# Expert gate and up weights loaded two column blocks at a time in 2 MB transfers, and the pieces taken in a new order

## What is computed

```python
    logits = (xt @ router).astype(jnp.float32)
    top_vals, top_idx = lax.top_k(logits, TOP_K)
    gates = jax.nn.softmax(top_vals, axis=-1)
    ...
    for e in range(N_EXPERTS):
        y_e = swiglu(xt, w_gate[e], w_up[e], w_down[e])
        y = y + combine[:, e:e + 1] * y_e.astype(jnp.float32)
```

## Time and profile before

| | |
|---|---|
| median of 3 runs | 1504.56 us (1502.7 to 1506.28) |
| profiled execution, first to last instruction | 1504.0 us |
| DVE busy | 1331.8 us, 89% |
| ACT busy | 1107.7 us, 74% |
| PE busy (its ends are modelled) | 1418.1 us, 94% |
| weights and other reads | 460.79 MB, 308 GB/s over the span |
| TensorE clock, mean granted | 0.981 |

### The profile page before, as it was taken

The page is one execution under the profiler, slowest core; times in us unless marked ns, Lnnn a source line. Parts: engine busy times, 40 slices in busy tenths (PEclk is TensorE's granted clock), DMA queues, the critical chain, the costliest instruction groups (busy, mean ns, idle before and its releaser), DMA issues.

```text
span 1504.0 us, 40039 instructions
## 1 busy us (share of the span) xinstructions
PE 1418.1 (94%) x17659; PEld 1161.2 (77%) x17659; DVE 1331.8 (89%) x1324; ACT 1107.7 (74%) x1036; POOL 111.0 (7%) x160
## 2 busy tenths in 40 slices
PE   7999999999999999899999999999999889898786
PEld 5888878888888788698687797788777776766663
DVE  4999987545569899899999999999999999999997
ACT  4797755444358676587897878888888888978884
POOL 2121014000043001200000000000000000000001
PEclk8999999999999999999999999999999999999898
DMA  9654466457554527879999999999999999999993
GB/s 316 237 168 155 162 235 219 141 183 236 171 180 141 172 87 270 345 304 380 405 413 392 412 411 397 411 409 394 411 407 410 412 406 411 411 401 410 411 396 132
DMA packets 141347, 464.86 MB, mean 309 GB/s; under 512 B 8234, under 2 KB 10410, under 8 KB 126800
## 3 DMA queue, kind: packets, MB, share of 16 engines
q1 hardware_dynamic: 138960, 457.21, 79.7%
q0 software_dynamic: 1920, 4.55, 1.0%
q10 hardware_dynamic: 288, 0.48, 0.1%
HBM read 460.79 MB, written 2.89 MB: 308 GB/s over the span
## 4 chain that ended last, share of the span: by engine, by line
PE 56%; DVE 29%; DMA 5%; issue 4%; ACT 3%; POOL 1%; SPq 1%; DVEq 0%; ACTq 0%
PE ps L859 17%; PE ps L860 17%; PE ps L861 17%; DVE w_lo L2274 13%; DVE w_lo L2277 6%; ACT w_hi L1655 2%; PE ps L972 2%; DMA x<-in_moe_w_gate 2%; DMA stage<-in_w_in 2%; DMA stage<-in_moe_w_up 1%; DVE w_lo L1746 1%; POOL x L786 1%; DVE arena L2292 1%; DVE arena L2312 1%; SPq L646 1%
## 5 line engine op out<-in xcount | busy, mean ns | idle before, releaser
L861 PE MATMUL ps<-arena,w_lo 128*128 128x128 f16 (+7 forms) x3952 | 568.9, 215 | 13.7 <-issue 13.6
L859 PE MATMUL ps<-arena,w_hi 128*128 128x128 f16 (+7 forms) x3952 | 569.1, 215 | 13.4 <-issue 6.6
L860 PE MATMUL ps<-arena,w_hi 128*128 128x128 f16 (+7 forms) x3952 | 569.1, 215 | 11.3 <-issue 11.3
L859 PEld LDWEIGHTS ps<-arena,w_hi 128*128 128x128 f16 x3952 | 388.3, 100 | 28.9 <-issue 16.9
L860 PEld LDWEIGHTS ps<-arena,w_hi 128*128 128x128 f16 x3952 | 388.2, 100 | 25.1 <-issue 16.5
L861 PEld LDWEIGHTS ps<-arena,w_lo 128*128 128x128 f16 x3952 | 388.2, 100 | 12.8 <-issue 6.9
L859 PE MATMUL ps<-xhl,w_hi 128*128 128x264 f16 x1120 | 312.0, 279 | 11.8 <-DVE w_lo L1746 4.6
L860 PE MATMUL ps<-xhl,w_hi 128*128 128x264 f16 x1120 | 311.9, 278 | 0.0
L861 PE MATMUL ps<-xhl,w_lo 128*128 128x264 f16 x1120 | 311.8, 278 | 0.0
L1746 DVE SCALAR_TENSOR_TENSOR w_lo<-stage,w_hi 128x2048 f16<-128x2048 f32 (+1 forms) x95 | 210.5, 2236 | 81.7 <-ACT w_hi L1352 81.4
L1352 ACT ACTIVATE w_hi<-stage 128x2048 f16<-128x2048 f32 (+1 forms) x95 | 174.5, 1853 | 88.1 <-PE ps L861 75.3
(11 more groups left out here) (345 smaller groups left out, 1937.1 us busy)
## 6 DMA issues: line engine op xcount, KB each, us to landing
stage<-in_moe_w_up SPq DMA_DIRECT2D x57, 1024.0 KB, 14.0
stage<-in_moe_w_down SPq DMA_DIRECT2D x56, 1024.0 KB, 14.4
stage<-in_w_in SPq DMA_DIRECT2D x43, 1024.0 KB, 5.5
mixer_only<-in_moe_w_up SPq DMA_DIRECT2D x39, 1024.0 KB, 13.1
stage<-in_moe_w_gate SPq DMA_DIRECT2D x33, 1024.0 KB, 8.4
arena<-in_moe_w_gate SPq DMA_DIRECT2D x32, 1024.0 KB, 13.4
mixer_only<-in_moe_w_gate SPq DMA_DIRECT2D x24, 1024.0 KB, 13.7
x<-in_moe_w_down SPq DMA_DIRECT2D x16, 1024.0 KB, 14.8
```

What stands on the lines that cost most here:

```text
L859: mm(out, ah, bh, start=start, stop=False, skip_group_check=True)
L860: mm(out, ah, bl, start=False, stop=False, skip_group_check=True)
L861: return mm(out, al, bh, start=False, stop=stop, skip_group_check=True)
```

## The change

Gate and up are now loaded two blocks side by side: one load holds 256 rows of the matrix and 2048 columns (blocks 0 and 1, 2 MiB) or 1536 columns (blocks 2 and 3, 1.5 MiB); a load of down holds 512 rows (2 MiB), which is two of its pieces. An expert is 23 loads (`LOADS`) instead of 42, into seven homes of 2 MiB instead of 14 of 1 MiB, and a load waits until the last piece that reads the load seven places back is converted (`LAST_OF`). The pieces that ACT, DVE and PE work on have the size and number they had, but since a load serves two blocks, these are taken in turns, and `visit_order` becomes: gate of blocks 0 and 1 in turns (m = 0 to 7), up of the two in turns (8 to 15), gate of blocks 2 and 3 in turns (16 to 21), down of 0 and 1 (22 to 29), up of 2 and then 3 (30 to 35), down of 2 and 3 (36 to 41). ACT's and DVE's steps on the hidden values move to fixed m. A gate or up piece's rows no longer lie side by side in its home. ACT still writes `w_hi` of such a piece in one instruction (two for block 3); DVE writes `w_lo` in one instruction for each group of 128 rows, which is two for blocks 0 to 2 and four for block 3. The expert's tokens for the next visit are gathered ahead of m = 36 (before: ahead of m = 40). `FP32_DOWN` is empty, so that nothing is multiplied unsplit. Some tensors are laid side by side in memory (`zx`, `mixer_xhl`) to make 2 MiB homes of them.

```diff
--- before.py
+++ after.py
-RING = 14
-
-
-TWICE = 5
-RING_ORDER = list(range(TWICE, 12)) + list(range(TWICE)) + [12, 13]
+
+BIG = 2 * PIECE
+HOMES_AFTER = [2, 3, 4, 0, 1, 5, 6]
...
+SIDE = [2048, D_EX - 2048]
 def visit_order():
...
+    def in_turn(kind, b):
+        return [(kind, i, q) for part in range(2) for i in (b, b + 1)
+                for q in range(part * n_pieces(i) // 2, (part + 1) * n_pieces(i) // 2)]
+
+    def whole(kind, *blocks):
+        return [(kind, i, q) for i in blocks for q in range(n_pieces(i))]
+
+    return (in_turn("g", 0) + in_turn("u", 0) + in_turn("g", 2) + whole("d", 0, 1) + whole("u", 2, 3)
+            + whole("d", 2, 3))
...
+LOADS = ([("g", 0, q) for q in range(4)] + [("u", 0, q) for q in range(4)] + [("g", 1, q) for q in range(4)]
+         + [("d", 0, c) for c in range(4)] + [("u", 1, q) for q in range(4)] + [("d", 0, c) for c in range(4, NC)])
...
+LAST_OF = [max(m for m in range(VISIT) if j in loads_of(m)) for j in range(NLOADS)]
+
+FP32_DOWN = ()
...
+        HOMES = [stage[:, (PRE + i) % SLOTS:(PRE + i) % SLOTS + 2, :].rearrange("p i c -> p (i c)") for i in (0, 2, 4)] + [
+            mixer_only[:, 0:BIG], landing, mixer_xhl[:, BIG:2 * BIG], zx[:, 0:BIG]]
...
+        def halves_of(at, m, to, both=False):
+
+            kind, b, q = order[m]
+            slot = to[:, (PRE + m) % SLOTS, :]
+            if kind == "d":
+                return [(load_home(at, loads_of(m)[0])[:, (q % 2) * PIECE:(q % 2 + 1) * PIECE], slot)]
+            width = 512 * len(BLOCKS[b])
+            c0, side = (BLOCKS[b][0] * 512) % 2048, SIDE[b // 2]
+            k = KT // n_pieces(b)
+            dst = slot.rearrange("p (two k c) -> p two k c", two=2, k=k)
+            if both:
+                return [(load_home(at, j)[:, 0:2 * side].rearrange("p (k n) -> p k n", k=2)[:, :, c0:c0 + width]
+                         .rearrange("p k (c two) -> p two k c", two=2), dst[:, :, 2 * i:2 * i + 2, :])
+                        for i, j in enumerate(loads_of(m))]
+            return [(load_home(at, j)[:, t * side + c0:t * side + c0 + width].rearrange("p (c two) -> p two c", two=2),
+                     dst[:, :, 2 * i + t, :]) for i, j in enumerate(loads_of(m)) for t in range(2)]
...
+            kind, side, q = LOADS[j]
             if kind == "d":
-                return (A["moe_w_down"][0, e, f + q * 256:f + q * 256 + 256, :]
-                        .rearrange("a (p k) n -> (a p) k n", p=P)), 2, D
+                return (A["moe_w_down"][0, e, q * 512:q * 512 + 512, :]
+                        .rearrange("a (q p k) n -> (a p) q (k n)", p=P, k=2)), PIECE
...
+                        if first and i < 9:
+                            new_home(i)
+                        elif i < 7:
+                            sp.wait_ge(*in_visit(bank_full, 5, (r, 0), -1))
                         else:
-                            sp.wait_ge(S["lo_done"], so_far((r, v), VISIT, split(n - RING + 1)))
-                        load(*visit_piece(e, m), n + v * VISIT + (0 if first else ROUND))
-
-            def new_home(m):
-
-                if m < SLOTS:
-                    sp.wait_ge(S["lo_done"], split(PRE + m - SLOTS + 1))
-                elif m == SLOTS:
+                            was = ((r, (i - 7) // NLOADS), (i - 7) % NLOADS)
+                            load_used(*was)
...
+                if i < 3:
+                    sp.wait_ge(S["lo_done"], split(PRE + 2 * i + 2 - SLOTS))
+                elif i == 3:
                     filled(sp, ("so", L - 1))
-                elif m == 9:
+                elif i == 4:
                     sp.wait_ge(S["out_dma"], 16 * 11 * L)
-                elif m == 10:
+                elif i in (5, 6):
+                    load_used((0, 0), i - 5)
...
+                for m, (kind, blk, q) in enumerate(order):
+                    if kind == "d":
+                        down(at, blk, q)
+                    else:
+                        gate_up(at, kind, blk, q)
+                    if m == 7:
+                        scatter(at, 0)
+                    if m == 11:
+                        scatter(at, 1)
+                    if m == 15:
+                        select_rows(at, first)
+                    if last and m == 25:
+                        residual_rows(0, [tokens_added(at, 1), in_visit(bank_free, 7, at, 0)])
+                    if m == FP32_FROM - 1:
+                        if last:
+                            residual_rows(1, [columns_read("u", 2, at), columns_read("g", 3, at)])
+                        else:
+                            gather((at[0], at[1] + 1), at)
...
+                if n >= PRE:
+                    for j in loads_of(n - PRE):
+                        act.wait_ge(*load_landed((0, 0), j))
+                    piece_done(act, n - SLOTS)
+                    hi_of((0, 0), n - PRE)
...
+                parts = halves_of(at, m, w_hi, True)
+                for src, dst in parts[:-1]:
+                    fn(dst, src, ACT.Copy, scale=WS)
+                src, dst = parts[-1]
+                fn(dst, src, ACT.Copy, scale=WS).then_inc(S["hi_done"], 1)
...
+            def lo_of(at, m):
+
+                parts = list(zip(halves_of(at, m, w_lo), halves_of(at, m, w_hi)))
+                for (src, dst), (_, hi) in parts[:-1]:
+                    V.scalar_tensor_tensor(dst, src, WS, hi, ALU.mult, ALU.subtract)
+                (src, dst), (_, hi) = parts[-1]
+                V.scalar_tensor_tensor(dst, src, WS, hi, ALU.mult, ALU.subtract).then_inc(S["lo_done"], 1)
...
+                    if m == 24:
+                        select((at[0], v + 1))
+                    if m == 33:
+                        hidden(at, 2, silu_e, silu_e)
+                    if m == 34 and split_all:
+                        hidden_lo(at, 2, silu_e)
+                    if m == 35:
+                        hidden(at, 3, h_fp32[:, 3:4, :], h_fp32[:, 3:4, :])
+                    if m == 36 and split_all:
+                        hidden_lo(at, 3, h_fp32[:, 3:4, :])
...
```

521 lines of the change are left out of this document (272 added, 249 removed).

## The result

The changed kernel takes 1549.07 us (median of 4 runs, 1546.99 to 1550.39) against 1504.9: ratio 1.0289, 95% interval 1.0274 to 1.0304. It is 44 us slower, and 7 us above the top of my range. The direction was right; the size was near double what I had forecast.

What follows compares the result with a forecast made beforehand. DVE was taken to bound visits 4 to 6, PE mainly visits 0, 2 and 3, DMA second. Terms 7.3 + 2.5 - 2.3 + 6.6 + 3.3 + 5 + 1 = +23.4 took 1504.6 to 1528 us; range 1505 to 1542.

Steps and rivals of the forecast that it cites:

- DVE's extra instructions: w_lo on DVE: 36 more instructions a visit at 0.068 us; +7.3 in visits 4 to 6, +2.5 in 1 and 3.
- The higher figure of the Trainium skill: Fixed latency per DVE instruction: about 150 cycles, 0.16 us; 288 added instructions would be an estimated 45 us before cover.
- The start: First expert load: ACT held 4.4 us with the merged parts behind it, PE covering about 1.1 us; +3.3 us.
- The visit's end: Visit boundaries: PE's six last down pieces wait for block 2's rest part, DVE then waits 1.1 us; +6.6 over six.
- the tail: After the last w_lo: PE ends 10.7 us behind DVE, 5.9 more than before; taken as +5 us, no cover.
- the clock: PE's granted clock falls after gaps ahead of m = 36 in light visits; +1 us in all.
- Loads: Longer rows land faster, so visit 7's load waits vanish: -2.3 us there; later-freed homes cost 0.
- rival 1: Expert visits: loads are the true bound, longer rows save 15 us and hide DVE's instructions; 1498 us, 8%.
- Rival 3: Visit boundaries: homes come late, each costs some 3 us more, 21 in all; 1549 us, 7%.
- the six boundaries of the forecast: Ends of visits where DVE was to wait 1.1 us; six of seven counted, one left to PE-bound cover.
- half cover: Visits 1 and 3: DVE's free 2.8 and 3.2 us cover half the added instructions' cost, leaving +2.5 us.
- The lower clock: Rival at m = 36: lower clock for three of six down pieces, 1.7 us in five visits, +8; 1536 us, 15%.

Runs made afterwards that it cites:

- the split alone: Kernel before, with DVE writing w_lo of gate and up pieces in two instructions (four for block 3), nothing else changed: 1512.49 us (1.0051).
- all places moved: Changed kernel's order with loads and homes of before, hidden steps and additions two conversions earlier, no PE wait for bank 2: 1508.14 us (1.0022).
- 1522.35: Changed kernel with both start edits, hidden steps and additions earlier, and paired homes filled block by block in two transfers: 1522.35 us (1.0104).
- 1519.89: Changed kernel with its large loads, both start edits, and hidden steps and additions earlier: 1519.89 us (1.0098).
- 1520.63: Changed kernel's order with small loads, hidden steps and additions earlier, no bank 2 wait, w_lo in two instructions (four for block 3): 1520.63 us (1.0117).

## Why the prediction was right in direction and too small

- **DVE's extra instructions** (+7.3 and +2.5, less 2.3 in visit 7): right in size, shown by the split alone, +7.5, with parts that partly make up for each other. The higher figure of the Trainium skill ("VectorE: DVE Perf Modes", the TRN2 errata) is excluded for instructions that follow one another: the two halves of a piece start 1.13 us apart, and 288 of them added 7.5 to 14 us, not 45. What I did not see is that the price is not a constant: it is 7.5 us in the kernel before, where it also buys off the load waits (visit 7 is 3.8 us shorter for it), and 12.5 to 14 us with all places moved, where visit 7 gained 0.3.
- **The start (+3.3): this step failed.** Undone, it gives 12.4 us, and PE was 13.6 us late. That ACT is held 4.4 us was nearly right (4.7). That PE "has about one piece's cover (1.1 us) when the merged parts are due" was wrong: there was none, 6 us of lateness at the merged parts were 7.7 at the end of the gathering. And the term ended the path there. It named the wrong end of the chain, because I compared PE's matmuls of the mixer and did not read what PE waits for ahead of its first expert piece. The bank 2 wait stands in the changed code and its releaser, the copy of the counts, stands in DVE's program behind a `w_lo`, so an order listing and the code together would have shown it: 3.4 us, and 2.8 more by the clock. And I counted visit 0 as cover for DVE's instructions ("PE hides it"), rightly, without seeing that a visit bound by PE has no cover for a late PE.
- **The visit's end (+6.6), the tail (+5) and the clock (+1)**, 12.6 together: the steps that I had named are the cause, as moving them alone gave back 14.7, which is near in size. The chain to DVE's wait was wrong. It stands at the first piece of the next visit at all seven boundaries (11.8 us, where I had 6.6 at the sixth), and at five of them without any wait for PE: it came through ACT, whose conversion of that piece stands behind block 3's rounded half and the next tokens. I had timed PE and DVE there and not ACT. The tail measured 6.5. The clock was mis-sized: it took 2.5 us at m = 36 in each of visits 5 and 6 and 1.7 in visit 1, the last of which I had left out.
- **Not costed at all:** PE's waits for the additions, 22.5 us where there were 8, worth 3.6 us at the end. And 3 us that stay of the order with all places mended (1508.14), whose cause is open.
- **Loads (rival 1 and 3).** ACT waits for no load in the expert part of the changed kernel, so the late homes cost nothing there, as I had put it. Rival 3 was right about the mechanism all the same: with one instruction per piece the smaller stock runs out and costs 12 to 14 us (1522.35 against 1508.14). What longer rows are worth no run isolates; visits 4 and 5 of the changed kernel ran at 412 and 414 GB/s, those of the kernel before at 409 and 410. The fixed cost of about 2 us that rival 1 takes from the Trainium skill ("DMA: Bandwidth & Descriptors", the anatomy of one DMA) stands there for transfers that GpSimd issues, and these are SP's; 19 fewer transfers a visit gained nothing here (1519.89 against 1520.63). That the kernel before waits for loads in visit 7 alone was misread: ACT waits 15.2 us for them there in visit 7 and 5.8 in visit 6; 4.75 us is DVE's free time. The load waits of visit 7 did vanish: it takes 107.6 us to the end of its last `w_lo`, 0.7 less than before, for DVE now waits for `w_hi` there instead; I had 2.3.

Visit by visit on PE, with the six boundaries of the forecast taken as those ahead of visits 1 and 3 to 7 (us):

| | forecast | measured |
|---|---|---|
| up to the end of visit 0 | 3.3 | 14.3 |
| visits 1 and 3 | 4.7 | 11.6 |
| visit 2 | 0 | 0.3 |
| visits 4 to 6 | 10.6 | 13.2 |
| visit 7 and the tail | 3.8 | 4.6 |
| clock, not placed | 1 | |
| sum | 23.4 | 44.0 |

Half of the miss is the start. A third lies in visits 1 and 3, where I had counted on half cover. There was none: the split alone made each of them 2.2 us longer on PE, and moving the hidden steps and the additions gave 3.8 back in visit 1.

The sum as the runs have it: 12.4 (start) + 14.7 (hidden steps) + 3.6 (additions) = 30.7, of which 29.2 were found when all were mended together (1549.1 to 1519.9); then 12.5 for the instructions (with 1 MiB loads in the place of the large ones, which changed 0.7), and 3.2 for the rest of the order. These steps lead from one kernel to the other, so they add up to 44 by their making; what the runs show is the size of each.

The lower clock was a rival of its own with 1536 for its time. It was no rival but a factor: it came on top behind the wait at the start and behind gaps of 6.4 us and more at m = 36 (in visit 7 hardly, 0.3 us), not behind those of 4.9 and less in visits 3 and 4, and went where the wait was taken away. No run changed the clock alone, so its share is read from the traces, not shown by an experiment.

## What to carry to other kernels

When a first load grows, follow it past the engine that waits for it: list for the engine that ends last every wait ahead of its first new instruction, with the place of each releaser in its own program, and see whether the stage behind has any cover. A step on which all of a later block waits belongs as early in the busy engine's program as its inputs allow; two conversions were worth more here (14.7 us) than the 36 instructions a visit (7.5 to 14). And the larger transfers were worth nothing here, where another engine was the bound; they forced 36 more instructions a visit onto just that engine, and a smaller stock of loads that shows once that engine is quick.

## What the chip showed that I had not expected

- A wait of PE cost more than its length. 3.4 us of waiting ahead of the first expert matmul were followed by some 5.7 us at the clock's lower level (0.50), and taking the wait away gave 6.3 us. Gaps of 6.4 and 7.1 us ahead of m = 36 in visits 5 and 6 were followed by 2.5 us lost, gaps of 2.9 and 3.9 us at the same places, with the hidden steps earlier, by none; but one of 7.1 us in visit 7 was followed by 0.3 alone, so the gap's length doesn't settle it. That is left open.
- A slower DVE made one visit faster: with 36 more instructions visit 7 took 104.5 us instead of 108.3, since the loads caught up: ACT's waits for loads went from 21.0 us in all to none.
- A step can wait in a ring: at the end of a visit ACT waits for DVE's product, and DVE then for the conversion that stands behind it in ACT's program.
